# Order of the query blocks within a pair of heads in a causal attention stage

## The reference

```python
for blk in range(seq // Q_BLOCK):            # 4 query blocks of 128
    q0 = blk * Q_BLOCK
    q1 = q0 + Q_BLOCK
    s = jnp.einsum("bhqd,bhkd->bhqk", qn[:, :, q0:q1], kn[:, :, :q1]) * scale
    s = s + cum[:, :, q0:q1, None] - cum[:, :, None, :q1]
    s = jnp.where(mask, s, -jnp.inf)
    p = jax.nn.softmax(s, axis=-1)
    outs.append(jnp.einsum("bhqk,bhkd->bhqd", p, vh[:, :, :q1]))
```

## Time and profile before

| | |
|---|---|
| median of three executions | 5022.51 us |
| the profiled execution, its own time | 5024.48 us |
| its span, first to last instruction | 5021.6 us |
| PE busy | 4594.5 us, 91% of the span |
| DVE busy | 2824.9 us, 56% |
| ACT busy | 1818.0 us, 36% |
| mean granted TensorE clock | 0.948 of full |
| attention steps of layer 0 and of layer 1 | from about 677 to 905 us, and from about 2055 to 2283 us |

### The profile page before, as it was taken

How to read it: one execution, slowest core, us unless ns; L and a number is a source line. 1 busy time by engine, 2 the same in 40 slices (tenths; PEclk the granted TensorE clock), 3 DMA queues, 4 the chain that set the end, 5 groups by cost and what they waited for, 6 DMA issues and landing times.

```text
span 5021.6 us, 65708 instructions
## 1 busy us (share of the span) xinstructions
PE 4594.5 (91%) x22507; PEld 3888.8 (77%) x22507; DVE 2824.9 (56%) x4620; ACT 1818.0 (36%) x2936; POOL 600.8 (12%) x631
## 2 busy tenths in 40 slices
PE   8999999999999999999999877897646899999999
PEld 7887787878878877878788766685535799999998
DVE  5436545454254365454542784453889666666666
ACT  3225334232232254343321322232229544444444
POOL 0000000000000000000000000000565322222221
PEclk9999999999999999999999967798869999999999
DMA  3222210222222222102222210031103677777776
GB/s 124 100 96 81 91 52 34 84 84 100 99 86 100 98 78 92 51 34 84 92 92 100 78 59 0 25 118 42 42 25 134 229 274 275 275 278 277 276 277 241
DMA packets 85577, 599.88 MB, mean 119 GB/s; under 512 B 10640, under 2 KB 11024, under 8 KB 18512
## 3 DMA queue, kind: packets, MB, share of 16 engines
q1 hardware_dynamic: 57456, 410.85, 22.4%
q0 software_dynamic: 27136, 162.28, 9.2%
q10 hardware_dynamic: 864, 25.17, 1.2%
HBM read 570.99 MB, written 27.26 MB: 119 GB/s over the span
## 4 chain that ended last, share of the span: by engine, by line
PE 69%; issue 14%; DVE 8%; ACT 4%; DVEq 3%; ACTq 1%; DMA 1%; POOLq 0%; POOL 0%; SPq 0%
PE PB L189 21%; PE PB L191 20%; PE PB L190 20%; ACT STG L2429 1%; PE PB L1990 1%; PE PB L897 1%; PE PB L886 1%; DVE NM L918 1%; PE PB L1091 1%; DVE PB L1874 1%; DVEq L1876 1%; DVEq L2288 1%; PE PB L1104 1%; DVE SC L2291 1%; ACT WH L162 1%
## 5 line engine op out<-in xcount | busy, mean ns | idle before, releaser
L189 PE MATMUL PB<-XH,WH 128*128 128x512 f32 (+1 forms) x3552 | 1359.6, 383 | 110.5 <-DVE WL L170 76.5
L190 PE MATMUL PB<-XL,WH 128*128 128x512 f32 (+1 forms) x3552 | 1347.2, 379 | 0.0
L191 PE MATMUL PB<-XH,WL 128*128 128x512 f32 (+1 forms) x3552 | 1347.1, 379 | 0.0
L170 DVE TENSOR_TENSOR WL<-RAW,WH 128x1024 fp32r<-128x1024 f32 x520 | 645.5, 1280 | 499.2 <-ACT WH L162 485.3
L189 PEld LDWEIGHTS PB<-XH,WH 128*128 128x128 f32 x3552 | 680.5, 192 | 226.2 <-issue 81.5
L190 PEld LDWEIGHTS PB<-XL,WH 128*128 128x128 f32 x3552 | 680.4, 192 | 106.1 <-issue 1.7
L191 PEld LDWEIGHTS PB<-XH,WL 128*128 128x128 f32 x3552 | 678.8, 191 | 104.4
L162 ACT ACTIVATE WH<-RAW 128x1024 fp32r<-128x1024 f32 x520 | 522.0, 1050 | 575.9 <-PE PB L191 551.2
L248 POOL TENSOR_TENSOR SQ<-SQ 128x512 f32<-128x512 f32 x49 | 71.7, 1463 | 2359.1 <-ACT SQ L231 2347.9
L189 PE MATMUL PB<-WH,WGH 128*128 128x512 f32 x768 | 299.5, 390 | 10.8 <-DVE WGL L2568 10.8
L191 PE MATMUL PB<-WH,WGL 128*128 128x512 f32 x768 | 302.0, 393 | 0.0
(11 more groups left out here) (399 smaller groups left out, 7557.5 us busy)
## 6 DMA issues: line engine op xcount, KB each, us to landing
RAW<-weights SPq DMA_DIRECT2D x387, 1024.0 KB
gate_matrix<-STG ACTq DMA_DIRECT2D x6, 4096.0 KB, 11.5
GM<-gate_matrix POOLq DMA_DIRECT2D x128, 192.0 KB, 5.3
X<-x SPq DMA_DIRECT2D x4, 512.0 KB, 5.4
UV<-rows,IDX POOLq DMA_INDIRECT x128, 5.7
out<-FIN SPq DMA_DIRECT2D x4, 512.0 KB, 2.6
MEMX<-mem POOLq DMA_DIRECT2D x1, 1024.0 KB, 5.1
SK<-sub_keys POOLq DMA_DIRECT2D x1, 1024.0 KB, 5.2
```

The costliest lines, as they stand in the source:

```text
L170: c.nc.vector.tensor_tensor(c.WL[p][:, cols], c.RAW[p][:, cols], c.WH[p][:, cols].bitcast(F32), ALU.subtract).then_inc(c.sem("w_split"), 1)
L189: c.nc.tensor.matmul(out, wh, xh, start=start, stop=False)
L190: c.nc.tensor.matmul(out, wh, xl, start=False, stop=False)
L191: return c.nc.tensor.matmul(out, wl, xh, start=False, stop=stop)
```

## The change

The list of steps is written in another order. Before, the first head's query blocks came in the order 0, 1, 2, 3 and then the second head's in the same order; the numbers of key blocks were 1, 2, 3, 4, 1, 2, 3, 4. After, even steps take the first head with rising query blocks and odd steps the second head with falling ones; the numbers of key blocks are 1, 4, 2, 3, 3, 2, 4, 1. The places of the weight splits and of the square, given by the step's index, stay as they are.

```diff
 PAIRS = HEADS // 2
-JS = [(hh, qb) for hh in range(2) for qb in range(QB)]
+JS = [(j % 2, j // 2 if j % 2 == 0 else QB - 1 - j // 2) for j in range(2 * QB)]
```

## The result

The changed kernel takes 5047.28 us (median of six runs, 5044.69 to 5049.65) against 5022.84 us for the kernel before in the same comparison: a ratio of 1.0049 with a 95% interval of 1.0036 to 1.0062. It is slower by 24 us. The forecast was 5010 us with a range up to 5029, so the time lies outside, on the side of the first rival.

The account below looks back on a forecast made before the run. PE, busy 91% of the span, was taken to bound the kernel through its waits and lower clock. 5024.5 - 7.7 (steps) - 4.8 (fewer low stretches) = 5012.0, so 5010 us for the median, range 5003 to 5029.

Parts of the forecast that it names:

- the first rival: Behind the steps, new waits give pairs two low stretches: 5026 or 5039 us; 0.12 above 5032, 0.23 (shared) for 5018-5030.
- The schedule of the steps: Inside the steps of each pair: token sums start 0.48 us earlier, 7.7 us over 16 pairs.
- The wait of 1.29 before turn 6: Late in the steps: PE waits 1.29 us for top 6, of four blocks, behind DVE's second split; the new longest.
- 0.44 before product 6: Late in the steps: PE waits 0.44 us because product 6 needs the copy of turn 6.
- the second term: Clock behind the steps of 14 pairs: 9 to 10 low stretches instead of 13, a gain of 4.8 us.
- low stretches: Behind the steps: clock at 0.50 (1.2 GHz) for some 3.4 us; 13 in 14 pairs, 1.61 us each.
- The slide: Clock fall comes ever later against the token sums, about 0.1 us a pair, 0.1 + 0.48 with the shorter pairs.
- Low stretches unchanged at 13: Rival, clock behind the steps: only the steps get shorter, -7.7 us, 5015; chance 0.20.
- steps that gain nothing: Rival, late steps: second split and copy 4 hold top 6 back 0.5 us more; 5022; within a shared 0.23.

Follow-up runs that it names:

- a_half: The changed kernel with two filler matmuls of 512 columns before turn 6 and none before product 6: 5013.6 us.
- a_late: The changed kernel with DVE's second split after the eighth copy instead of after copy 4: 4994.9 us.
- a_fill: The changed kernel with seven filler matmuls of 512 columns in its new waits, five before turn 6 and two before product 6: 5013.1 us.
- a_front: The changed kernel with DVE's two splits at steps j = 0 and 1 instead of 2 and 3: 5026.3 us.
- b_late: The kernel before, in its old order, with DVE's second split after the eighth copy: 5031.9 us.
- b_shift: The kernel before, in its old order, with DVE's two splits each one step later, at j = 3 and 4: 5060.7 us.
- b_fill: The kernel before with five filler matmuls of 512 columns in its waits (two before turn 6, two before turn 7, one before product 7): 5018.7 us.

## Why the prediction was wrong

**The schedule of the steps was right.** 0.48 us a pair was put down. From a pair's first scores to its token sums, in the changed kernel where the clock did not fall inside the steps, and in the kernel before:

```profile
707.07 0.38 PE L1091 MATMUL PB<-KZ,QZ 128*128 128x128 f32 x2
...
722.04 1.90 PE L1104 MATMUL PB<-CT,SQ 128*128 128x2 f32 x16
```

```profile
736.74 0.38 PE L1091 MATMUL PB<-KZ,QZ 128*128 128x128 f32 x2
...
752.15 1.90 PE L1104 MATMUL PB<-CT,SQ 128*128 128x2 f32 x16
```

That is 14.97 and 15.41 us, a gain of 0.44, the same as 28.98 - 28.54 by the whole pairs of a_half. The wait of 1.29 before turn 6 and of 0.44 before product 6 are there: in the forecast turn 6 came 749.11 - 738.00 = 11.11 us after the six projection matmuls began, and in the trace it is 747.99 - 736.88, the same 11.11. That the split ahead of the top holds it back is shown by a_late; the share of the longer copy was not tested by itself.

**The step that failed is the second term, the count of low stretches.** The prediction took the slide of the fall against the pair as all that decides it, and so reached 9 or 10 from 13, a gain of 4.8 us. In the same 14 pairs 30 were measured (34 against 14 over the whole attention), a loss of 20 x 1.6 = 32 us. The slide is real, though the rows that the prediction reads it from do not give it: 754.70 - 752.15 = 2.55 and 816.10 - 813.50 = 2.60, from two views and the edges of chosen windows, are 0.05 us apart in two pairs, not 0.2. The clock record does give it: the falls start at 754.6 and 816.1, 30.7 us a pair, where the pairs last 30.6. And a_half and a_fill, whose pairs have the length that was forecast, have 11 and 10 stretches and take 5013.6 and 5013.1 us, 12 below the kernel before, which is the forecast's own sum. But it holds only while the late part of the steps is busy enough. The wait of 1.29, computed by the prediction itself, ends 2.6 us before the token sums (749.11 and 751.67) and takes that away: a_fill, which fills it and leaves the schedule as it is, brings the ten back.

**The first rival was the mechanism, and it was undersized twice.** It was given two low stretches a pair at most, and six of the fourteen pairs have three, and in those the fall comes before the last products are done, so that the token sums run at the lower clock too, 3.31 instead of 1.74 us. That this slow sparse work is what prolongs the low clock is likely and was not tested. And it was said that the last pair of a layer, without token sums, has none; the changed kernel has two behind it in each layer, from 910.0 and 2302.7 us. Its price per stretch was right: (5046.7 - 5021.6 + 16 x 0.44) / 20 = 1.6 us, with what moved outside the attention left out. Its chance, 0.12 for a time clearly slower, was too small: the rows showed the clock falling behind a far milder stretch in 11 of 14 pairs, and the change made exactly that stretch sparser. The rule of the Trainium skill that was set beside it, "TensorE: Matmul & The Clock Gate", section "A second HAM failure mode: psum-queue depth-cycling", warned of this: by it, frequent short idles of PE between groups of matmuls make the clock swing. The changed kernel against a_fill agrees. Read as a matter of how many idles there are, a_front does not: it has four in a pair where the changed kernel has two, and 15 low stretches against 34. Read against the longest late wait, it agrees with all three.

**The other rivals.** Low stretches unchanged at 13, and steps that gain nothing, are both excluded by the trace: 34, and the 0.44 us a pair.

**Left open.** What in the late steps has to be how busy for the clock to stay up was not measured on its own; a_half shows that a wait of about 0.75 us there is harmless in this kernel and 1.2 is not. By the brackets of the traces, where waits come out some 0.2 us shorter, the longest wait of the late steps and the count of low stretches go together roughly: 0.34 us and 14 (before), 0.39 and 5 (a_late), 0.49 and 11 (a_half), 0.87 and 20 (b_late), 1.02 and 34 (changed), 1.23 and 33 (b_shift); the length of the pair differs between them too. Why b_fill's median is 8 us above its profiled run is open as well.

## What to carry to other kernels

Once a hand schedule shows where PE waits, look at what stands next to the longest wait: beside small matmuls, one wait of 1.2 us cost about 2 us a pair here through the clock (20 low stretches of 1.6 us over 16 pairs), four times what the reordering gained. Put long waits away from the small matmuls (a_front: more waiting in sum, 15 low stretches and not 34), or fill them, at best with work that has to be done anyway. An order of work and the place of side work (here the weight split) are one decision: each of them alone cost time, both together gained 30 us.

## What was not expected of the hardware

At the lower clock the sixteen token sums, with two columns each, take 3.31 us and not 1.74, so almost the full factor of two: small matmuls suffer as much as wide ones (512 columns: 0.43 against 0.23 us from start to start). The weight load of 128 columns that goes with each of them takes 0.33 us and not 0.19; that the loads bound these matmuls is likely and was not tested. And very little work keeps the clock up: two matmuls of 512 columns a pair, 0.45 us in a wait of 1.2 (a_half), were worth 34 us over the kernel. With every wait of the steps filled (a_fill) the clock still fell ten times, behind small matmuls alone.
